# Dividing the second attention's result by transfers instead of by a transposition: stored reciprocal sums, a late product, a fifth score bank, and scores of both heads in a row

## What is computed

```
score = sum_h iw * relu(iq @ ik.T)            # indexer, masked by chunks
_, sel = top_k(score, 256)                    # keys that a query may see
s = (q @ k[sel].T) * 64**-0.5 + bias[rel]     # hidden keys: -inf
p = softmax(s)                                # exp(s - max) / sum(exp(s - max))
bo = (p @ v[sel]) * silu(bg)
y = concat(ao, bo) @ w_out ;  out = rmsnorm(x + y)
```

## Time and profile before

| | |
|---|---|
| median of 3 runs | 741.91 us (740.95 to 744.52) |
| the profiled execution | 741.63 us |
| its span (first to last instruction) | 739.8 us |
| mean granted clock of TensorE | 0.997 of full speed |
| busy over the span: PE, DVE, ACT, POOL | 97%, 83%, 44%, 49% |
| from the first score matmul of the second attention to the first matmul of the output projection | 519.7 to 643.4 us |
| busy between 560 and 570 us: PE, DVE, ACT, POOL | 9.73, 9.59, 7.60, 9.11 of 10 us |
| last chain of work, share of PE | 85% |
| three matmuls of 128x512 of the output projection, first start to fourth | 0.69 us |
| two steps of the second attention, a long and a short one | 6 to 8 us |

### The profile page before, as it was taken

The page is one execution under the profiler, slowest core; times in us unless marked ns, Lnnn a source line. Parts: engine busy times, 40 slices in busy tenths (PEclk is TensorE's granted clock), DMA queues, the critical chain, the costliest instruction groups (busy, mean ns, idle before and its releaser), DMA issues.

```text
span 739.8 us, 12056 instructions
## 1 busy us (share of the span) xinstructions
PE 720.9 (97%) x4184; PEld 602.1 (81%) x4184; DVE 615.8 (83%) x1293; ACT 322.6 (44%) x723; POOL 366.1 (49%) x445
## 2 busy tenths in 40 slices
PE   8999999999999999999999999999899999999996
PEld 7757888888888898999888888888787878788886
DVE  5678999999997979898599999999689898646554
ACT  7547131131313666667531131314777767522222
POOL 5220222223556859771135555547999999612210
PEclk9999999999999999999999999999999999999999
DMA  7340211212220010113021112220010112312231
GB/s 282 113 143 20 57 44 44 57 43 57 68 62 1 1 43 2 43 31 100 16 70 44 47 39 57 53 76 1 30 44 10 50 46 89 127 57 95 78 113 58
DMA packets 24564, 44.58 MB, mean 60 GB/s; under 512 B 3076, under 2 KB 10936, under 8 KB 24376
## 3 DMA queue, kind: packets, MB, share of 16 engines
q1 hardware_dynamic: 23336, 42.76, 19.5%
q10 hardware_dynamic: 1168, 1.05, 0.4%
HBM read 35.40 MB, written 6.57 MB: 57 GB/s over the span
## 4 chain that ended last, share of the span: by engine, by line
PE 85%; DVE 5%; POOL 4%; issue 2%; DMA 2%; ACT 1%; SPq 0%; POOLq 0%; DVEq 0%; ACTq 0%
PE psum L1273 41%; PE psum L1494 12%; PE psum L1356 5%; PE psum L1368 4%; PE psum L1334 4%; PE psum L1337 4%; PE psum L1383 3%; PE psum L1228 3%; PE psum L1211 3%; PE psum L1193 2%; PE psum L1165 2%; DMA xs<-in_x 1%; PE psum L1341 1%; PE psum L1340 1%; DVE probs L1761 1%
## 5 line engine op out<-in xcount | busy, mean ns | idle before, releaser
L609 POOL TENSOR_TENSOR w_lo<-w_raw,w_hi 128x512 fp32r<-128x512 f32 x60 | 77.5, 1294 | 215.5 <-ACT w_hi L807 215.2
L1640 DVE MATCH_REPLACE8 score<-top,score 128x640 f32<-128x640 f32 (+5 forms) x176 | 157.4, 906 | 0.0
L1635 DVE MAX8 top<-score 128x8 f32<-128x640 f32 (+5 forms) x176 | 148.7, 910 | 1.1
L807 ACT ACTIVATE w_hi<-w_raw 128x512 fp32r<-128x512 f32 x60 | 37.4, 629 | 209.8 <-PE psum L1273 206.8
L983 ACT ACTIVATE probs<-psum,small 128x384 f32<-128x384 f32 (+7 forms) x128 | 94.8, 741 | 38.4 <-DVE small L1700 30.0
L1273 PE MATMUL psum<-big_hi,w_hi 128*128 128x512 f32 x256 | 99.7, 389 | 0.0
L1273 PE MATMUL psum<-big_hi,w_lo 128*128 128x512 f32 x256 | 99.6, 389 | 0.0
L1273 PE MATMUL psum<-big_lo,w_hi 128*128 128x512 f32 x256 | 99.6, 389 | 0.0
L1273 PE MATMUL psum<-w_hi,big_hi 128*128 128x512 f32 x192 | 74.7, 389 | 0.0
L1273 PE MATMUL psum<-w_lo,big_hi 128*128 128x512 f32 x192 | 74.7, 389 | 0.0
L1273 PE MATMUL psum<-w_hi,big_lo 128*128 128x512 f32 x192 | 74.7, 389 | 0.0
(11 more groups left out here) (195 smaller groups left out, 1630.7 us busy)
## 6 DMA issues: line engine op xcount, KB each, us to landing
w_raw<-in_w_in SPq DMA_DIRECT2D x62, 256.0 KB, 2.6
xs<-in_x SPq DMA_DIRECT2D x8, 512.0 KB, 7.0
k_high_twice<-k_high_twice SPq DMA_DIRECT2D x16, 256.0 KB, 3.7
xres<-in_x SPq DMA_DIRECT2D x8, 512.0 KB, 4.3
out_y<-y_out SPq DMA_DIRECT2D x8, 384.0 KB, 2.9
w_tail<-in_w_out SPq DMA_DIRECT2D x10, 256.0 KB, 2.6
bias_scratch<-bias_row SPq DMA_DIRECT2D x1, 2304.0 KB
bias<-bias_scratch SPq DMA_DIRECT2D x12, 128.0 KB, 3.0
```

Of the source, the lines that this page charges most:

```text
L609: pool.tensor_tensor(lo[:, 0:cols], w_staged(n)[:, 0:cols], hi[:, 0:cols].bitcast(f32), ALU.subtract).then_inc(w_lo_made, 1)
L807: act.activation(w_parts(n)[0][:, 0:cols], w_staged(n)[:, 0:cols], ACT.Copy).then_inc(w_hi_made, 1)
L1635: ins = dve.max(top8[:, i - SEL0, :], sc)
L1640: ins = dve.match_replace(sc, top8[:, i - SEL0, :], sc, TAKEN)
```

## The change

- `share`, `turn_shares` and `scale_gate` are gone. `invert` writes the reciprocals of both heads to `rinv` as before. SyncE stores the 128x2 of them to a row in DRAM (`store_sums`, elements of 4 bytes) and loads each head's row back to 64 partitions (`load_shares`, two transfers). There are four slots for it.
- VectorE multiplies the finished product by this late (`scale_mix`, four steps behind), out of SBUF and into SBUF. `finishB` multiplies by the gate alone. In an iteration whose step t is short, `invert` now stands behind the score work of step s + 1, and `scale_mix` behind that; else `scale_mix` comes first, and `invert` before the score work.
- The scores have a fifth bank, the one that the transposed sums had.
- TensorE's order: quads 0 and 1, the scores of both heads, quads 2 and 3, weigh.
- SyncE's loop runs over the 32 steps. `copy_keys(1, b + 1)` stands at piece 5 of a block, behind `store_sums` of that step, and the weight chunks at steps of their own.
- GpSimd's split of mixB waits for `mixB_scaled`.

```diff
-        S_BANKS, BACK_BANK, O_BANK, T_BANK = (4, 4), 4, 5, 6
+        S_BANKS, O_BANK, T_BANK = (4, 5), 5, 6
...
-            for b in range(1, BLOCKS):
-                copy_keys(1, b)
-                for n in range(CHUNKS + 3 + (0, 1, 3)[b - 1], CHUNKS + 3 + (1, 3, 6)[b - 1]):
-                    load_chunk(n)
-            for n in range(CHUNKS + 9, CHUNKS + 2 * DB):
+            def store_sums(s):
+                c = 2 * s % 8
+                sp.wait_ge(sums_inverted, s + 1)
+                if s >= 4:
+                    sp.wait_ge(shares_loaded[s % 4], 32 * (s // 4))
+                sp.dma_start(bass.AP(sum_rows, s % 4 * 2 * P, [[1, P], [P, 2]]), rinv[:, c:c + 2],
+                             allow_slow_non_contiguous=True
+                             ).then_inc(shares_stored[s % 4], 16)
+            def load_shares(s):
+                sp.wait_ge(shares_stored[s % 4], 16 * (s // 4 + 1))
+                if s >= 4:
+                    sp.wait_ge(mixB_scaled, s - 3)
+                for m in range(2):
+                    sp.dma_start(shares[m * HEAD:(m + 1) * HEAD, s % 4, :],
+                                 bass.AP(sum_rows, (s % 4 * 2 + m) * P, [[0, HEAD], [1, P]])
+                                 ).then_inc(shares_loaded[s % 4], 16)
+            for s in range(STEPS):
+                b, piece = divmod(s, TILES)
+                store_sums(s)
+                if s >= 1:
+                    load_shares(s - 1)
+                if piece == 5 and b + 1 < BLOCKS:
+                    copy_keys(1, b + 1)
+                for k, (after, split_at) in enumerate(OUT_TIMES):
+                    if s == after * TILES + split_at + 2:
+                        load_chunk(CHUNKS + 3 + k)
+            load_shares(STEPS - 1)
+            for n in range(CHUNKS + 3 + sum(b * TILES + piece + 2 < STEPS for b, piece in OUT_TIMES),
+                           CHUNKS + 2 * DB):
                 load_chunk(n)
...
-                pool.wait_ge(o_moved, STEPS + last_step(t) + 1)
+                pool.wait_ge(mixB_scaled, last_step(t) + 1)
...
+            def scale_mix(s):
                 b, i = place_of(1, s)
                 g = mixB[:, b, i * P:(i + 1) * P]
+                dve.wait_ge(o_moved, STEPS + s + 1)
+                dve.wait_ge(shares_loaded[s % 4], 32 * (s // 4 + 1))
+                dve.tensor_tensor(g, g, shares[:, s % 4, :], ALU.mult).then_inc(mixB_scaled, 1)
...
-                if 1 <= s <= STEPS:
-                    invert(1, s - 1)
-                    share(s - 1)
+                few = len(qs) == 2
+                if s >= SHARE_LAG and not few:
+                    scale_mix(s - SHARE_LAG)
                 if s >= 2:
                     finishB(s - 2)
                 turned(1, qs)
+                if qs and not few:
+                    invert(1, s - 1)
                 if s + 1 < STEPS:
                     for m in range(2):
                         far_min(1, s + 1, m)
                         soften(1, s + 1, m)
-                if 1 <= s <= STEPS:
-                    scale_gate(s - 1)
+                if few:
+                    invert(1, s - 1)
+                    if s >= SHARE_LAG:
+                        scale_mix(s - SHARE_LAG)
```

More of the change, by code:

```diff
@@ L149, in build @@
     w_tail, _ = place("w_tail", [P, 2, WIDTH], f32, at=w_hi_at + 2 * ROW)
-    shares, _ = place("shares", [P, 2, HEAD], f32, at=o_tmp_at)
+    shares, _ = place("shares", [P, 4, P], f32, at=o_tmp_at)
     lam4, _ = place("lam4", [P, 4, HEAD], f32, at=mask_at + 4096)
@@ L201, in build @@
         scratch = nc.dram_tensor("bias_scratch", [P * (A_HEADS + B_HEADS) * RELS], f32, kind="Internal")
+        sum_rows = nc.dram_tensor("sum_rows", [4 * 2 * P], f32, kind="Internal")
         compact = nc.dram_tensor("bias_row", [(A_HEADS + B_HEADS) * RELS], f32, kind="Internal")
@@ L266, in build @@
         o_moved = sem("o_moved")
-        shares_made = sem("shares_made")
-        shares_turned = sem("shares_turned")
-        gate_scaled = sem("gate_scaled")
+        sums_inverted = sem("sums_inverted")
+        shares_stored = [sem(f"shares_stored{r}") for r in range(4)]
+        shares_loaded = [sem(f"shares_loaded{r}") for r in range(4)]
+        mixB_scaled = sem("mixB_scaled")
         o_squared = sem("o_squared")
@@ L465, in build @@
         LATE = CHUNKS + len(OUT_TIMES)
+        SHARE_LAG = 4
         WARM_TURNS, BETWEEN = 36, (4, 5)
@@ L1387, in weigh_heads @@
                             ins.then_inc(pv_done, 1)
[L1389 to L1394, removed]
             def turn_mix(t):
@@ L1440, in attend_chosen @@
                     qs = quads[1, t] if t >= 0 else []
-                    long = len(qs) == 4
-                    for quad in qs[0:1 if long else 2]:
+                    for quad in qs[0:2]:
                         turn(1, t, quad)
@@ L1449, in attend_chosen @@
                             pe.transpose(bank(T_BANK + 1)[:, 0:P], ident[:, :], ident[:, :])
[L1450 to L1453, removed]
                     if s + 1 < STEPS:
                         scores(1, s + 1, 1)
[L1456 to L1459, removed]
+                    for quad in qs[2:4]:
+                        turn(1, t, quad)
                     if s == STEPS - 1:
@@ L1480, in _ @@
                     if t == 0 and half == 0:
-                        pe.wait_ge(gate_scaled, STEPS)
+                        pe.wait_ge(exp_done, bank_user(4) + 1)
                     elif t == 0:
@@ L1735, in invert @@
                 dve.wait_ge(exp_done, 2 * (ph * STEPS + s) + 2)
-                inverted[ph, s] = later(dve.reciprocal(rinv[:, c:c + 2], rsum[:, c:c + 2]))
+                if ph == 0:
+                    inverted[ph, s] = later(dve.reciprocal(rinv[:, c:c + 2], rsum[:, c:c + 2]))
+                    return
+                if s >= 4:
+                    dve.wait_ge(shares_stored[s % 4], 16 * (s // 4))
+                dve.reciprocal(rinv[:, c:c + 2], rsum[:, c:c + 2]).then_inc(sums_inverted, 1)
             def turned(ph, quads):
@@ L1810, in _ @@
                               ALU.not_equal, ALU.mult).then_inc(last_mask_made, 1)
[L1811 to L1825, removed]
             def finishB(s):
@@ L1830, in finishB @@
                 g = mixB[:, b, i * P:(i + 1) * P]
-                dve.wait_ge(gate_scaled, s + 1)
                 dve.wait_ge(pv_done, quads_through(1, s))
                 dve.tensor_tensor(g, bank(O_BANK)[:, 0:P], g, ALU.mult).then_inc(o_moved, 1)
+            def scale_mix(s):
+                b, i = place_of(1, s)
+                g = mixB[:, b, i * P:(i + 1) * P]
+                dve.wait_ge(o_moved, STEPS + s + 1)
+                dve.wait_ge(shares_loaded[s % 4], 32 * (s // 4 + 1))
+                dve.tensor_tensor(g, g, shares[:, s % 4, :], ALU.mult).then_inc(mixB_scaled, 1)
             def mix_low(t):
@@ L1862, in _ @@
                         soften(1, s + 1, m)
-                if 1 <= s <= STEPS:
-                    scale_gate(s - 1)
+                if few:
+                    invert(1, s - 1)
+                    if s >= SHARE_LAG:
+                        scale_mix(s - SHARE_LAG)
                 if STEPS - 1 <= s <= STEPS:
                     mix_low(s - STEPS + 1)
+            for s in range(STEPS + 2 - SHARE_LAG, STEPS):
+                scale_mix(s)
             for t in range(TILES + 1):
```

## The result

The changed kernel took **825.83 us** (median of 4, 823.53 to 830.03) beside 741.93 of the kernel before: ratio 1.1135, interval 1.1089 to 1.118. It is slower, as forecast, but by 84 us and not by 15; that is 60 us beyond the upper end of the range.

What follows compares the result with a forecast made beforehand. TensorE, busy 97% of the span, was taken as the bound. Savings -8.6, GpSimd's key wait -0.9, late keys +18.0, clock +5.1 and end +2.1 gave +15.7 on 741.6: 757 us, range 748 to 766.

Steps and rivals of the forecast that it cites:

- rival 2: VectorE's scale_mix waits for the reciprocals' store and loads, the store landing in 1.5 us: 8 to 16 us more, chance 0.14.
- The late keys: At three block boundaries TensorE waits 6.0 us for key copies queued behind the reciprocals' store: 18.0 us added.
- The clock: After each of TensorE's three stops the clock falls to half speed, costing 1.7 us each: 5.1 us added.
- The savings: What TensorE saves, (a) to (d) together: 8.6 us.
- (a): In the second attention, 32 transpositions of sums go from TensorE, 24 of them saving 0.11 us each: 2.6 us.
- (b): Both heads' scores in a row save TensorE one turn from transposition to score in 15 long iterations: 1.5 us.
- (c): TensorE no longer waits for the spread sums before transposing them, at five places: 2.5 us saved.
- (d): At the start, a fifth score bank spares TensorE the wait for the first exponential and slow clock: 2.0 us saved.
- rival 1: Key copies stay hidden, not slower: only the last block's savings count, 740.5 us, or 732 where GpSimd gets ahead; chance 0.08.
- The end: In the output projection TensorE waits for GpSimd's split of chunk 14, late behind weight chunk 11: 2.1 us added.
- VectorE's product of two SBUF tiles: The product replacing scale_gate takes 9 to 30 us for 32, against 30 before, costing nothing while TensorE has the stops.

Runs made afterwards that it cites:

- before_two: The kernel before, also storing and loading back reciprocals that nobody reads, with the loads two steps behind the stores: 796.2 us (1.0711).
- four_stores: The changed kernel without the reciprocals' stores from step 4 on, loads waiting only for the first store of their slot: 769.05 us (1.0376).
- four_stores_keys: The changed kernel without the reciprocals' stores from step 4 on and with key copies issued one step sooner: 752.23 us (1.0143).
- no_transfers: The changed kernel without any store or load of sums, VectorE multiplying by an always present tile (the identity) instead: 742.36 us (1.000).

## Why the prediction was wrong

- **The step that failed** is the price of the store, in rival 2: "By rows the small store landed within 33.87 - 32.40 = 1.5 us". That row is the store of `band` into `bias_row`, whole rows; the new one writes 256 neighbouring elements of 4 bytes and took 7.8 us. The sum of the forecast held nothing for it or for VectorE's wait behind it, which came to 59.4 us. The text said that "no row here shows a store of single elements" and still used 1.5 with a microsecond to spare; the honest upper bound was unknown. Rival 2 was the right mechanism for VectorE, priced at 8 to 16 us and given 0.14. The 28 stores from step 4 on are worth 825.83 - 769.05 = 56.8 us, by VectorE's wait and by what they hold back together.
- **What was missing altogether**: that such a store delays transfers that have nothing to do with it, in its own queue and in others. No rival had it, and `before_two` shows it costing over 50 us where nobody reads the data, together with the waits of SyncE's queue for its own stores and loads.
- **The late keys** (6.0 us a stop, 18.0, and 5.1 of clock, together 23.1) were right in place and nearly in the length of the stops where the store is out of the way: three stops, 15.5 us. With the clock they were worth 16.8 (`four_stores` against `four_stores_keys`, which still has one such wait of 2.6 us). In the changed kernel they are 27.2 us: the copies are issued later, behind loads that wait for stores, and land later (4.4 us against 3.4).
- **The clock**, 1.7 us a stop, came to 1.7 at one stop, of 3.2 us. In the changed kernel the stops are many, and from 540 to 560 us the granted clock was 0.74 on the mean.
- **The savings.** (a), (b) and (c), 6.6 us or 1.65 a block, were 0.98, 0.96 and 1.37 in the last three blocks; (d), 2.0 by the forecast, came with the first step to 2.9. That makes 4.0 by the end of the first block and 3.3 in the other three, 7.3 in all for 8.6. A part of what is missing is VectorE's copy of a quad, for which TensorE now waits longer: 2.0 us in 8 waits against 1.0 in 4. The rest is open. None of it reaches the end, and this the forecast saw only in rival 1: "only the last block's savings count" is what `no_transfers` measured (742.36 for 740.5). In the forecast's own case, with TensorE stopped for 23 us, GpSimd is ahead and the savings count; so this is no fault of its sum, but it says that the change had about a microsecond to win while GpSimd's work stayed as it was. GpSimd's share of busy time over the stage, over 9 of 10, pointed there.
- **The end**: 2.1 us forecast (its own figures, 650.2 and 647.9, give 2.3), 10.4 measured behind GpSimd (L774), and 2.6 in `four_stores`. The size is the store's doing again.
- **VectorE's product of two SBUF tiles**, bounds 9 and 30 us for 32: 13.4 in the changed kernel, 426 ns each; 17.5 in `no_transfers`, 584 ns. On the mean the product costs more than with an input in PSUM, but about half of the 952 ns of the earlier trace rows: neither bound is a price, since it depends on how often GpSimd is at work. In the changed kernel the one at 540.23 us took 1.13 us, while GpSimd subtracted two SBUF tiles (539.95, 1.26 us); the one at 548.41, while GpSimd stood still, took 0.29. By the Trainium skill's rule on two SBUF inputs beside GpSimd ("SBUF — State Buffer", "Who interferes with whom") one blocks the other; these two products agree with it.

```profile
L1847 DVE TENSOR_TENSOR mixB<-mixB,shares 128x128 f32<-128x128 f32 x32 | 13.4, 426 | 59.4 <-DMA shares<-sum_rows 59.4
```

The 84 us in the order of the edits: stores 56.8, late keys 16.8, the first four stores with 64 loads and the chunks behind them 9.9 (752.23 to 742.36; 9.4 of it is the one stop behind those four stores and its clock), and 0.4 between that and the kernel before. The edits were made one upon the other, so these are shares of one path, not the price of each alone.

Still open is why neighbouring elements of 4 bytes are slow, whether it matters that the same rows are being read, and how far apart is enough: 8 bytes gave 3.6 us, 256 gave 2.0, nothing between was run. Open too is by what the store holds back others. The traces show only that its own packets are over at once (one store, below) and that those of a chunk behind it then trickle (one chunk of `before_two`, above).

## What to carry over

A transfer's price comes from a row with the same pattern, not the same size; where there is none, measure it by itself, with nobody waiting, and look at what lands beside it as well. A round trip through the device's memory is put on a path only where latency, the rate of the queue that issues it, and the other transfers of that queue have each been counted. And before adding up what one engine saves, follow the chain of the engine that feeds it: here TensorE waited for GpSimd's keys once, 0.87 us, and yet GpSimd was the floor.

## What the hardware showed

The slow store's own data move at once, and its landing comes long after. Of the store issued at 535.74 us the packets ran between 536.6 and 537.6 (289 under 512 bytes; by their number its 256 elements are among them); then the DMA engines did nothing up to 540.4, and the store's loads could be issued at 544.26. The packets of these two stretches of the changed kernel:

```profile
DMA packets 353, 0.03 MB, mean 34 GB/s; under 512 B 289, under 2 KB 353, under 8 KB 353
```

```profile
DMA packets 0, 0.00 MB, mean 0 GB/s; under 512 B 0, under 2 KB 0, under 8 KB 0
```

So the DMA engines' busy share says little of such a cost: it was 0.13 and 0.07 in the stretches from 520 to 560 us, and 0.77 from 565.2 to 570, when a weight chunk had just been issued behind the stores and only 29 GB/s moved. The time from issue to landing does.
